# First two weight chunks computed together, bias rows and memory tokens handled earlier, two exponentials joined

## The chip, the cores and the metric

One core of a Trainium2 chip. The metric is the device time of one execution in microseconds; lower is better. A transformer trunk of four layers runs from HBM to HBM in one launch.

## What is computed

The reference is a trunk of four layers on 256 tokens of width 1024, all in float32. Cut to what the opening of the first layer does:

```python
p = x @ attn_w_in[j]                     # 1024 -> 3*768 + 256
q, k, v = jnp.split(p[..., :2304], 3, -1)
bias = table[_t5_bucket(k_pos[None, :] - q_pos[:, None])]
probs = jax.nn.softmax(q_h @ k_h.T + bias)      # 6 heads, 2 maps each
w = probs[:, 0] - lam * probs[:, 1]
km, vm = jnp.split(mem @ w_kv, 2, -1)           # 256 memory tokens
recalled = softmax(qx @ km.T) @ vm              # 4 memory heads
y = jnp.concatenate([mixed, recalled], -1) @ w_o[layer]
x = layer_norm(ALPHA * x + y)
f = conv_ffn(x); x = layer_norm(ALPHA * x + f)
```

Layers 1 and 2 replace the attention by a gated recurrence and by a short convolution; layer 3 is attention again.

## The kernel before

**Tiling.** Every projection is cut into chunks of 256 output columns (or, for `O` forms, 256 rows); one chunk is 1 MB of weights and two *units* of 128 x 1024 numbers. SP streams the units in order into a ring of five buffers, `raw` (line 341); `load_unit(u)` at 599 fills one. Each float32 operand is split in two: ACT rounds a unit to `w_hi` (`round_unit`, 1025 to 1030), DVE subtracts to get `w_lo` (`lo_unit`, 1261 to 1267). Each product is then three passes on TensorE: hi by hi, hi by lo, lo by hi. `x` and the memory tokens are split the same way, a quarter at a time ("cut", ACT 1141 to 1146, DVE 1425 to 1430), into `xT_hi`, `xT_lo`, `memT_hi`, `memT_lo`.

**Order.** `make_schedule` (64 to 230) writes one list of items by hand. Every engine walks the same list and does its own part of each item, in the order of the list, so an item that waits on an engine holds all later items of that engine. `chunk(...)` (83) puts in the rounding of a unit two chunks ahead, the first half of the products, what stands in `between`, the rounding of the next unit, the second half, what stands in `after`. The dictionary `at` says what goes where: `at[2n]` is between the halves of the n-th chunk after the first, `at[2n + 1]` behind its second half. In layer 0 the chunks are 0 `XQ` (memory queries), 1 and 2 `QK` (queries and keys of heads 0 and 1), 3 `KM` and 4 `VM` (keys and values of the memory), 5 and 6 `QK` of heads 2 and 3, and so on. Chunk c has units 2c and 2c + 1.

**The opening.** SP issues a quarter of x and a quarter of chunk 0 in turn, four times (603 to 607), then units 2 to 4, with two small tables (the one-hot matrix and the bias table) ahead of unit 4 (608 to 612). From unit 5 on (628 to 656) a load waits until the `w_lo` of the unit five before is done. Behind some of these loads stand others: the memory tokens `y_tok` (1 MB) behind unit 5, the small tables one by one behind units 8 to 14 (`load_small`), the last of them `lam_w`; a write of the bias rows to a scratch in HBM behind unit 11 and the spread load of `bias` behind unit 13, which waits for that write.

PE warms up with `WARM_UP` = 2 products of zeros (860 to 866). Chunk 0 is made quarter by quarter (758 to 772): each quarter needs its x and its weights ("begin", ACT 1147 to 1151, DVE 1431 to 1436). The first half of chunk 1 has its own form (773 to 781): all hi passes, then the lo pass. `bias_rows` (898 to 902 on PE, 1191 to 1194 on ACT) is one product of the bias table with the one-hot matrix, copied to SBUF by ACT; it uses a side bank of PSUM that chunk 2 uses next, so chunk 2 waits for ACT's copy (`side`, 667 to 672). Its place is between the halves of chunk 1, `at[0]`. The memory tokens are cut between the halves of chunk 2, `at[2]`; chunk 3 waits for all four quarters (line 695).

**Memory attention and first heads.** Both `xlog` items (memory logits, PE 903 to 913, maxima on DVE 1492 to 1509) stand between the halves of chunk 4, `at[6]`. `xexp` 0 (four exponentials on ACT, 1195 to 1208) stands behind chunk 4, `at[7]`; `xexp` 1 and then `xprob` 0 (DVE, 1510 to 1526) between the halves of chunk 5, `at[8]`. `log` 0 and `log` 1 (logits of two heads, PE 914 to 924, DVE with the bias 1499 to 1509) stand behind chunk 5, `at[9]`; they reuse the PSUM banks of the memory logits and so wait for `xexp` 0 and 1. `exp` 0, `xturn` 0 (memory probabilities turned on PE 925 to 937, copied by ACT 1209 to 1216) and `xprob` 1 are `at[10]`, between the halves of chunk 6; `exp` 1 and `xpv` 0 (memory values, PE 947 to 958, reads ACT's copies) are `at[11]`. The rounding of units 14 and 15 (chunk 7) stands around the first half of chunk 5. `prepare` (`at[5]`, DVE 1389 to 1418 with two exponentials on ACT) makes constants from all small tables and waits until the last has landed.

Of the kernel before, what the change touches and what calls it, by code (L numbers as in the profile page):

```python
# [25 lines left out]
P = 128  # L26
SEQ = 256
D = 1024
KT = D // P
# [34 lines left out]
def make_schedule():  # L64
# [40 lines left out]
    for q in range(4):  # L105
        items.extend([("cut", "x", q), ("begin", q)])
    for u in range(2, AHEAD):
        split_units(u)
    norms = 0
    for layer in range(DEPTH):  # L110
# [3 lines left out]
        if layer == 0:  # L114
            split_units(1 + AHEAD)
        if kind == "attn":
# [16 lines left out]
            if layer == 0:  # L133
# [5 lines left out]
                at[0], at[2] = [("bias_rows",)], [("cut", "mem", q) for q in range(4)]  # L139
                at[5] = [("prepare",)]  # L140
# [92 lines left out]
def trunk_kernel(nc, stream, x, x_t, mem_t, rel_bias, ln, lam, subln, lower, hnorm, cconv, fconv,  # L233
# [93 lines left out]
    with ExitStack() as ctx:  # L327
# [145 lines left out]
        first_landed = [sem("first_landed0"), sem("first_landed2")]  # L473
# [124 lines left out]
        def _(sp):  # L598
# [4 lines left out]
            for q in range(4):  # L603
                at = slice(q % 2 * 512, q % 2 * 512 + 512)
                sp.dma_start(x_tok[:, q // 2, at], xT_dram[:, q // 2, at]).then_inc(xT_landed[q], 16)
                sp.dma_start(raw[:, q // 2, at], stream[0, :, q * 512:(q + 1) * 512]).then_inc(
                    raw_landed[q // 2] if q % 2 else first_landed[q // 2], 16)
            for u in range(2, RAW):
                if u == RAW - 1:
                    for dst, src in small[:2]:  # L610
                        sp.dma_start(dst[:], src).then_inc(table_landed, 16)
                load_unit(u)
# [53 lines left out]
        def _(pe):  # L666
# [13 lines left out]

            def half(c, i, pos, begun=False):
# [6 lines left out]
                if (c, i) == (1, 0):  # L688
                    pe.wait_ge(hi_ready, 3)
                elif c:  # L690
# [67 lines left out]
                elif c == 0:  # L758

                    banks, every = [PROJ[0][:, j * SEQ:(j + 1) * SEQ] for j in range(2)], slice(0, SEQ)  # L760
                    for q in (2 * i, 2 * i + 1):
                        pe.wait_ge(*(hi_ready, i + 1) if q % 2 else (first_hi, i + 1))
                        for w, a, part in ((w_hi, a_hi, cut_hi), (w_hi, a_lo, cut_lo), (w_lo, a_hi, None)):
                            if part:
                                pe.wait_ge(part["x"], q + 1)
                            else:
                                pe.wait_ge(*(lo_ready, i + 1) if q % 2 else (first_lo, i + 1))
                            for k in (2 * q, 2 * q + 1):
                                for j in range(2):
                                    at = (k % 4 * 2 + j) * P  # L770
                                    last = pe.matmul(banks[j], w[:, slot, at:at + P], a(k, every), start=(part is cut_hi and k + j == 0),
                                                     stop=(w is w_lo and k == KT - 1), skip_group_check=True)
                elif (c, i) == (1, 0):

                    bank, every = PROJ[1][:, 0:SEQ], slice(0, SEQ)
                    for k in range(KT):
                        pe.matmul(bank, w_hi[:, slot, k * P:(k + 1) * P], a_hi(k, every), start=(k == 0), stop=False)
                        pe.matmul(bank, w_hi[:, slot, k * P:(k + 1) * P], a_lo(k, every), start=False, stop=False)
                    pe.wait_ge(lo_ready, 3)
                    for k in range(KT):  # L780
                        last = pe.matmul(bank, w_lo[:, slot, k * P:(k + 1) * P], a_hi(k, every), start=False, stop=(k == KT - 1))
# [927 lines left out]
```

## Time and profile before

| | |
|---|---|
| median of 3 runs | 1250.84 us (1249.69 to 1251.08) |
| the profiled execution | 1250.47 us, its span 1248.7 us |
| granted TensorE clock, mean | 0.998 of full speed |
| PE busy | 1235.7 us, 99% of the span |
| DVE busy | 1024.2 us, 82% |
| ACT busy | 729.7 us, 58% |
| DMA | 229 MB, mean 184 GB/s |

PE is TensorE's matmuls, PEld its weight loads, DVE VectorE, ACT ScalarE, SPq the queue of SyncE that issues the transfers. In a timeline row the columns are start and duration in us, engine, line, operation, output and inputs, shapes, count of merged instructions, and in brackets how long the engine stood idle before and what ended that. "issue" means that the profile shows nothing that the engine waited for. A matmul's end is modelled, so its duration includes the way through the array; the distance of starts is the pace.

### The profile page before, as it was taken

The numbers are of one execution on the slowest core, as the hardware profiler recorded it, in microseconds if no ns is written. First come the engines' busy times: TensorE is split into PE (matmuls) and PEld (weight loads), VectorE is DVE, ScalarE is ACT, GpSimd is POOL, SyncE is SP. The second block draws the span as 40 slices with busy tenths as digits, with TensorE's granted clock in tenths as the row PEclk, the third lists the DMA queues.
The fourth block names the chain that finished last, engine by engine and source line by source line (L and its number), as shares of the span: only waits on it lengthen the run. The fifth ranks groups of instructions, "written<-read, shape, count | busy, mean of one in ns | idle before, by whom it ended". The sixth has DMA issues, their size and how long they took to land.

```text
span 1248.7 us, 19664 instructions
## 1 busy us (share of the span) xinstructions
PE 1235.7 (99%) x7368; PEld 1082.9 (87%) x7368; DVE 1024.2 (82%) x1597; ACT 729.7 (58%) x1188; POOL 20.0 (2%) x29
## 2 busy tenths in 40 slices
PE   8999999999999999999999999999999999999997
PEld 6888888888999998888889888888888888888886
DVE  6776888888879888988888878988888776988887
ACT  6665755555776546655554545655554774755552
POOL 0000000000000000000000000000000000000000
PEclk9999999999999999999999999999999999999999
DMA  9744575556454345666555665665555533666651
GB/s 337 236 146 135 183 245 187 190 186 191 154 185 133 121 137 168 224 197 200 188 187 169 221 204 168 221 202 189 192 189 172 188 119 118 204 218 202 193 193 54
DMA packets 64106, 229.27 MB, mean 184 GB/s; under 512 B 7526, under 2 KB 9190, under 8 KB 62860
## 3 DMA queue, kind: packets, MB, share of 16 engines
q1 hardware_dynamic: 64012, 228.02, 55.6%
q8 instruction: 59, 0.97, 0.3%
q14 instruction: 35, 0.29, 0.1%
HBM read 226.93 MB, written 1.06 MB: 183 GB/s over the span
## 4 chain that ended last, share of the span: by engine, by line
PE 95%; DMA 2%; DVE 1%; ACT 1%; SPq 0%; issue 0%; DVEq 0%
PE pair L753 28%; PE acc L853 21%; PE pair L756 14%; PE pair L791 4%; PE pair L792 4%; PE pair L793 4%; PE acc L753 2%; PE acc L834 2%; PE acc L832 2%; PE acc L833 2%; PE pair L1012 2%; DMA raw<-in_stream 1%; PE pair L816 1%; PE pair L820 1%; PE pair L818 1%; PE acc L756 1%
## 5 line engine op out<-in xcount | busy, mean ns | idle before, releaser
L1266 DVE TENSOR_TENSOR w_lo<-raw,w_hi 128x1024 fp32r<-128x1024 f32 x402 | 485.3, 1222 | 108.7 <-ACT w_hi L1030 107.2
L1030 ACT ACTIVATE w_hi<-raw 128x1024 fp32r<-128x1024 f32 x402 | 422.7, 1058 | 216.5 <-PE pair L756 69.8
L753 PE MATMUL pair<-xT,w_hi 128*128 128x512 f32 x1520 | 478.3, 396 | 1.5 <-ACT bias_rows L1193 1.5
L756 PEld LDWEIGHTS pair<-xT,w_lo 128*128 128x128 f32 x1520 | 285.8, 188 | 66.8
L756 PE MATMUL pair<-xT,w_lo 128*128 128x256 f32 x1520 | 298.9, 278 | 0.0
L753 PEld LDWEIGHTS pair<-xT,w_hi 128*128 128x128 f32 x1520 | 233.9, 189 | 4.9 <-issue 2.0
L1077 ACT ACTIVATE hid<-pair 128x512 f32<-128x512 f32 x88 | 52.5, 596 | 125.0 <-PE pair L756 125.0
L791 PE MATMUL pair<-xT,w_hi 128*128 128x256 f32 x344 | 100.3, 292 | 0.0
L1307 DVE TENSOR_TENSOR hid<-pair,hid 128x512 f32<-128x512 f32 x88 | 60.7, 690 | 47.3 <-ACT hid L1077 47.2
L792 PE MATMUL pair<-xT,w_hi 128*128 128x256 f32 x344 | 97.4, 283 | 0.0
L793 PE MATMUL pair<-xT,w_lo 128*128 128x256 f32 x344 | 97.3, 283 | 0.0
L853 PE MATMUL acc<-w_hi,gT_hi 128*128 128x512 f32 x304 | 94.0, 391 | 0.0
L853 PE MATMUL acc<-w_hi,gT_lo 128*128 128x512 f32 x304 | 93.7, 389 | 0.0
L853 PE MATMUL acc<-w_lo,gT_hi 128*128 128x512 f32 x304 | 93.7, 389 | 0.0
L1130 ACT ACTIVATE cv<-hid,fconv_w 128x256 f32<-128x256 f32 x176 | 79.2, 499 | 16.3 <-DVE hid L1307 16.0
L1283 DVE SCALAR_TENSOR_TENSOR cv<-hid,fconv_w,cv 128x255 f32<-128x255 f32 x176 | 77.4, 481 | 3.1
L1279 DVE SCALAR_TENSOR_TENSOR cv<-hid,fconv_w,cv 128x255 f32<-128x255 f32 x176 | 77.0, 480 | 0.0
L791 PEld LDWEIGHTS pair<-xT,w_hi 128*128 128x128 f32 x344 | 65.8, 191 | 3.3 <-issue 3.0
L853 PEld LDWEIGHTS acc<-w_lo,gT_hi 128*128 128x128 f32 x304 | 57.1, 188 | 12.2
L853 PEld LDWEIGHTS acc<-w_hi,gT_lo 128*128 128x128 f32 x304 | 57.1, 188 | 11.8
L792 PEld LDWEIGHTS pair<-xT,w_hi 128*128 128x128 f32 x344 | 65.9, 192 | 0.0
L793 PEld LDWEIGHTS pair<-xT,w_lo 128*128 128x128 f32 x344 | 65.8, 191 | 0.0
(221 smaller groups left out, 1661.1 us busy)
## 6 DMA issues: line engine op xcount, KB each, us to landing
raw<-in_stream SPq DMA_DIRECT2D x402, 512.0 KB, 4.6
gains<-in_ln SPq DMA_DIRECT2D x8, 1024.0 KB, 8.3
bias<-bias_scratch SPq DMA_DIRECT2D x2, 1152.0 KB, 8.6
x_tok<-in_x_t SPq DMA_DIRECT2D x4, 256.0 KB, 5.2
raw<-in_stream SPq DMA_DIRECT2D x4, 256.0 KB, 5.4
y_tok<-in_mem_t SPq DMA_DIRECT2D x1, 1024.0 KB, 10.2
x_tok<-in_x SPq DMA_DIRECT2D x1, 1024.0 KB, 6.7
out<-x_tok SPq DMA_DIRECT2D x4, 256.0 KB, 2.0
```

What stands on the lines that cost most here:

```text
L753: pe.matmul(bank, w_hi[:, slot, kk * P:(kk + 1) * P], xT[:, kk].rearrange("p a s -> p (a s)"), start=(kk == 0), stop=(kk == KT - 1), skip_ ...
L756: last = pe.matmul(bank[:, 0:SEQ], w_lo[:, slot, kk * P:(kk + 1) * P], xT[:, kk, 0, :], start=False, stop=(kk == KT - 1), skip_group_check ...
L791: pe.matmul(bank, w_hi[:, slot, at], a_hi(k, every), start=(k == 0), stop=False)
L792: pe.matmul(bank, w_hi[:, slot, at], a_lo(k, every), start=False, stop=False)
L793: last = pe.matmul(bank, w_lo[:, slot, at], a_hi(k, every), start=False, stop=(k == KT - 1))
L853: last = pe.matmul(ACC[2 * t + h][:], b(i, tok), w[:, slot, h * 512:h * 512 + 512], start=False, stop=False, skip_group_check=True)
L1030: nc.scalar.activation(w_hi[:, u % SPLIT, :], raw[:, u % RAW, :], ACT.Copy).then_inc(hi_ready, 1)
L1130: last = nc.scalar.activation(cv[:, w, i, :], hid[:, w, i, :], ACT.Copy, scale=fconv_w[:, layer, 1, first + i:first + i + 1])
L1266: v.tensor_tensor(w_lo[:, u % SPLIT, :], raw[:, u % RAW, :], w_hi[:, u % SPLIT, :].bitcast(F32), ALU.subtract).then_inc(lo_ready, 1)
L1279: last = v.scalar_tensor_tensor(dst[i][:, 1:SEQ], src[i][:, 0:SEQ - 1], weights(0, i), dst[i][:, 1:SEQ], ALU.mult, ALU.add)
L1283: last = v.scalar_tensor_tensor(dst[i][:, 0:SEQ - 1], src[i][:, 1:SEQ], weights(2, i), dst[i][:, 0:SEQ - 1], ALU.mult, ALU.add)
L1307: v.tensor_tensor(hid[:, w], PAIR[proj_ord[c] % 2][:, :, 0:SEQ], hid[:, w], ALU.add).then_inc(hid_ready, 1)
```

## The change

The units of chunks 0 and 1 are laid out anew: unit 0 holds the first half of the inner dimension of chunk 0, unit 1 that of chunk 1, units 2 and 3 the second halves. SP issues, for each quarter of x, that quarter and two quarter loads (256 KB each), one of each chunk; the two small tables follow all twelve, then unit 4. ACT and DVE cut x and round both quarters as they come. PE makes the products of a quarter for chunk 0 and chunk 1 in turn; the last quarter of chunk 1 falls in chunk 1's own halves. One warm-up product of half width is added. `bias_rows` stands ahead of chunk 1's first half, behind the rounding of unit 5. The memory tokens are cut behind chunk 1, ahead of the rounding of unit 8. `xexp` 1 stands directly behind `xexp` 0, ahead of the rounding of unit 14.

```diff
     for q in range(4):
-        items.extend([("cut", "x", q), ("begin", q)])
-    for u in range(2, AHEAD):
-        split_units(u)
+        items.extend([("cut", "x", q), ("begin", q, 0), ("begin", q, 1)])
...
             split_units(1 + AHEAD)
+            items.append(("bias_rows",))
...
-                at[0], at[2] = [("bias_rows",)], [("cut", "mem", q) for q in range(4)]
-                at[5] = [("prepare",)]
+                at[1], at[5] = [("cut", "mem", q) for q in range(4)], [("prepare",)]
+                at[8].remove(it("xexp", 1))
+                at[7].append(it("xexp", 1))
...
                 sp.dma_start(x_tok[:, q // 2, at], xT_dram[:, q // 2, at]).then_inc(xT_landed[q], 16)
-                sp.dma_start(raw[:, q // 2, at], stream[0, :, q * 512:(q + 1) * 512]).then_inc(
-                    raw_landed[q // 2] if q % 2 else first_landed[q // 2], 16)
-            for u in range(2, RAW):
-                if u == RAW - 1:
-                    for dst, src in small[:2]:
-                        sp.dma_start(dst[:], src).then_inc(table_landed, 16)
+                for u in (q // 2 * 2, q // 2 * 2 + 1):
+                    sp.dma_start(raw[:, u, at], stream[u // 2, :, u % 2 * UNIT + at.start:u % 2 * UNIT + at.stop]).then_inc(
+                        raw_landed[u] if q % 2 else first_landed[u], 16)
+            for dst, src in small[:2]:
+                sp.dma_start(dst[:], src).then_inc(table_landed, 16)
+            for u in range(4, RAW):
                 load_unit(u)
...
+            HI, LO = [(w_hi, xT_hi), (w_hi, xT_lo)], [(w_lo, xT_hi)]
+
+            def first_products(q, b, w, a):
+
+                slot, n = 2 * (q // 2) + b, 2 * (q // 2) + b + 1
+                if w is w_lo:
+                    pe.wait_ge(*(lo_ready, n) if q % 2 else (first_lo, n))
+                else:
+                    pe.wait_ge(*(hi_ready, n) if q % 2 else (first_hi, n))
+                    pe.wait_ge((cut_hi if a is xT_hi else cut_lo)["x"], q + 1)
+                for k in (2 * q, 2 * q + 1):
+                    for j in range(2):
+                        at = (k % 4 * 2 + j) * P
+                        last = pe.matmul(PROJ[b][:, j * SEQ:(j + 1) * SEQ], w[:, slot, at:at + P], a[:, k, :],
+                                         start=(w is w_hi and a is xT_hi and k + j == 0),
+                                         stop=(w is w_lo and k == KT - 1), skip_group_check=True)
+                return last
...
+                elif c < 2:
+
+                    for q, b in {(0, 0): [(0, 0), (0, 1), (1, 0), (1, 1)], (0, 1): [(2, 0), (2, 1), (3, 0)], (1, 0): [(3, 1)],
+                                 (1, 1): [(3, 1)]}[c, i]:
+                        for w, a in {(1, 0): HI, (1, 1): LO}.get((c, i), HI + LO):
+                            last = first_products(q, b, w, a)
...
             idle_work(WARM_UP)
+            pe.matmul(ACC[0][:, 0:SEQ], zeros[:, 0:P], zeros[:, 0:SEQ], start=True, stop=True)
...
-                    u, h = item[1] // 2, item[1] % 2
+                    u, h = item[1] // 2 * 2 + item[2], item[1] % 2
```

The last edit stands on ACT and on DVE; the two old forms of the first chunks' products (lines 758 to 781) go, and the layout of the stream on the host follows.

## Rows read from the trace of the kernel before

**Rows 1.** The page, part 4: the chain of work that ended last, by engine

```profile
PE 95%; DMA 2%; DVE 1%; ACT 1%; SPq 0%; issue 0%; DVEq 0%
```

**Rows 2.** All waits of PE over the span: total us, times, longest

```profile
PE pair L771 <- ACT w_hi L1151: 1.8, 3, 0.9
PE pair L753 <- ACT bias_rows L1193: 1.5, 1, 1.5
...
PE pair L791 <- issue: 1.0, 1, 1.0
PE acc L921 <- ACT ex L1205: 0.5, 1, 0.5
```

**Rows 3.** Timeline of PE, 0 to 60 us

```profile
1.51 3.78 PE L863 MATMUL acc<-zeros 128*128 128x512 f32 x4 [1.51 <-DVE zeros L1422]
...
22.32 0.70 PE L753 MATMUL pair<-xT,w_hi 128*128 128x512 f32 x2 [1.53 <-ACT bias_rows L1193]
...
29.17 0.36 PE L791 MATMUL pair<-memT_hi,w_hi 128*128 128x256 f32 x1 [1.04 <-issue]
...
50.20 1.13 PE L921 MATMUL acc<-qk 64*128 64x256 f32 x8 [0.53 <-ACT ex L1205]
...
58.07 1.08 PE L955 MATMUL pair<-xprobT,vm 128*64 128x256 f32 x8
```

**Rows 4.** Timeline of ACT, 12 to 60 us

```profile
14.11 1.06 ACT L1030 ACTIVATE w_hi<-raw 128x1024 fp32r<-128x1024 f32 x1 [0.51 <-DMA raw<-in_stream]
...
20.65 1.06 ACT L1030 ACTIVATE w_hi<-raw 128x1024 fp32r<-128x1024 f32 x1 [2.56 <-DMA raw<-in_stream]
...
22.85 1.06 ACT L1030 ACTIVATE w_hi<-raw 128x1024 fp32r<-128x1024 f32 x1 [0.67 <-DMA raw<-in_stream]
...
47.16 1.07 ACT L1030 ACTIVATE w_hi<-raw 128x1024 fp32r<-128x1024 f32 x1
48.11 0.48 ACT L1205 ACTIVATE ex<-acc,neg_max 128x256 f32<-128x256 f32 x1
...
49.91 1.09 ACT L1030 ACTIVATE w_hi<-raw 128x1024 fp32r<-128x1024 f32 x1
...
54.59 0.51 ACT L1205 ACTIVATE ex<-lg,neg_max 128x256 f32<-128x256 f32 x1 [2.10 <-DVE neg_max L1509]
...
56.58 1.06 ACT L1215 ACTIVATE xprobT<-pair 128x512 f32<-128x512 f32 x2
```

**Rows 5.** Windows: us, busy of PE, PEld, DVE, ACT, POOL, PEclk, DMA share, GB/s

```profile
4.00:6.00 2.00, 1.29 (x2) 0.00 (x0) 0.69 (x1) 1.11 (x2) 0.00 (x0) 1.00 0.86 192
6.00:8.00 2.00, 1.70 (x12) 1.50 (x12) 1.30 (x2) 1.36 (x3) 0.00 (x0) 1.00 1.01 371
14.00:16.00 2.00, 2.00 (x19) 2.00 (x18) 1.65 (x2) 1.46 (x2) 0.00 (x0) 1.00 1.05 418
18.00:36.00 18.00, 15.43 (x113) 14.37 (x112) 11.47 (x13) 10.34 (x17) 0.00 (x0) 1.00 1.03 369
```

**Rows 6.** Timeline of SP's queue, 20 to 45 us

```profile
26.69 0.33 SPq L600 DMA_DIRECT2D raw<-in_stream  x1
...
30.61 0.71 SPq L619 DMA_DIRECT2D lam_w<-in_lam  x1
```

**Rows 7.** Timeline of DVE, 20 to 54 us

```profile
23.94 1.23 DVE L1266 TENSOR_TENSOR w_lo<-raw,w_hi 128x1024 fp32r<-128x1024 f32 x1 [0.98 <-ACT w_hi L1030]
...
26.58 2.49 DVE L1430 TENSOR_TENSOR memT_lo<-y_tok,memT_hi 128x512 fp32r<-128x512 f32 x4
...
38.87 0.69 DVE L1392 CAST masks<-masks_in 128x1024 uint8<-128x1024 f32 x1 [4.18 <-DMA lam_w<-in_lam]
...
48.27 1.23 DVE L1266 TENSOR_TENSOR w_lo<-raw,w_hi 128x1024 fp32r<-128x1024 f32 x1 [0.42 <-ACT w_hi L1030]
...
51.03 1.23 DVE L1266 TENSOR_TENSOR w_lo<-raw,w_hi 128x1024 fp32r<-128x1024 f32 x1 [0.19 <-ACT w_hi L1030]
```

**Rows 8.** The chain of work in order of time: start us, us, what

```profile
51.65 0.12 PE pair L792
```

More of the change, by code:

```diff
@@ L472, in trunk_kernel @@
         xT_landed = [sem(f"xT_landed{q}") for q in range(4)]
-        first_landed = [sem("first_landed0"), sem("first_landed2")]
+        first_landed = [sem(f"first_landed{u}") for u in range(4)]
         cut_hi, cut_lo = [{"x": sem(f"x_{name}"), "mem": sem(f"mem_{name}")} for name in ("hi", "lo")]
@@ L686, in half @@
                 held = form == "O" and index[0] == chunks_of_sum - 2
-                if (c, i) == (1, 0):
-                    pe.wait_ge(hi_ready, 3)
-                elif c:
+                if c > 1:
                     pe.wait_ge(lo_ready, 2 * c + (2 if final or c in early else i + 1))
@@ L757, in half @@
                                              start=False, stop=(kk == KT - 1), skip_group_check=True)
[L758 to L781, printed above, removed]
+                elif c < 2:
[3 more added lines that the diff above has]
+                            last = first_products(q, b, w, a)
                 elif form == "F":
@@ L1431, in _ @@
                 elif name == "begin":
-                    u, h = item[1] // 2, item[1] % 2
+                    u, h = item[1] // 2 * 2 + item[2], item[1] % 2
                     at = slice(h * 512, h * 512 + 512)
@@ L1647, in stream_layout @@
         cols = {"QK": (P * index, MIX + P * index), "CG": (MIX + P * index, 2 * MIX + P * index)}.get(role)
-        if c == 0:
-            stream[c] = w[:, col:col + 256].reshape(KT, P, 256).transpose(1, 0, 2).reshape(P, 2 * UNIT)
+        if c < 2:
+            for i, first in enumerate(cols or (col, col + P)):
+                block = w[:, first:first + P].reshape(2, KT // 2, P, P).transpose(2, 0, 1, 3)
+                for h in range(2):
+                    stream[h].reshape(P, 2, KT // 2, 2, P)[:, c, :, i] = block[:, h]
             continue
```

## The prediction

> **What bounds the kernel now.** The page comes first. Its chain of the work that ended last is 95% TensorE (PE) [rows 1], so what a change is worth is how much PE idle time it takes out or puts in. The list of what PE waited for, over the whole span, names few places [rows 2]: the first products wait for rounded weights (1.8 us in three waits), chunk 2 for the copy of the bias rows (1.5), chunk 3 for "issue" (1.0), and the second set of head logits for an exponential (0.5). The last of these places is at 50.20, so PE runs without a wait from there to the end, and a microsecond won or lost ahead of it arrives whole. The edits touch only this opening, and the four lines hold 4.8 us, so about 5 us (0.4%) is all there is to win.
>
> PE's own timeline gives their places: 1.53 us before 22.32, 1.04 before 29.17, 0.53 before 50.20 [rows 3]. Then the other engines are read over the same stretch, and they decide. ACT rounds unit 6 at 20.65 and unit 7 at 22.85, both the moment their transfers land [rows 4]; the DMA engines are full from 18 to 36 us (share 1.03) [rows 5]. SP issues lam_w, the last small table, at 30.61 [rows 6], and DVE, which needs all small tables for "prepare", stands 4.18 us until it lands at 38.87 [rows 7]. Unit 12's low part and the memory logits' maxima stand behind "prepare" in DVE's order, the exponentials on ACT behind the maxima, the probabilities on DVE behind those. **From 38.87 to about 58 us a DVE-and-ACT chain that starts with a DMA landing runs close under PE.** It touches PE at 50.20 and stays just hidden at 58.07 (no wait is shown there).
>
> **The change, part by part.**
>
> *First two chunks together.* No product is added or removed; 96 of 0.12 us each [rows 8] are reordered so that each quarter of x feeds 24 instead of 12. ACT and DVE trade two whole-unit roundings for four half-unit ones each. SP issues four 256 KB transfers in place of two of 512 KB. All transfers keep their place by bytes in the one queue, so the last quarter lands about where unit 3 landed, 14.11 [rows 4]. From there 24 products (2.9 us) and the bias product put the start of chunk 2 at about 18.5 to 19, against 22.32: some 3.5 us earlier.
>
> The unshown price is that of one megabyte fetched in 2 KB pieces. Upper bound: the rate at which the first quarters crawled, 192 GB/s from 4 to 6 us, against 418 later with larger pieces: 5.5 minus 2.5 us, 3.0 later. Lower bound: a gain of 0.3, as I see no row that excludes finer pieces getting through sooner. The nearest row is 6 to 8 us, where quarters alone moved at 371: 2.8 minus 2.5, **0.3 us later** [rows 5]. I take that, since the four pieces come after this stretch; everything behind them in the queue shifts with them, lam_w too.
>
> *One more warm-up product*, half as wide: a quarter of the 3.78 us that the two present ones take, 0.95 [rows 3]. It lies in the idle time of 0.9 before the first product [rows 2]; without that cover it would cost 0.95.
>
> *Bias rows right behind.* ACT's copy no longer stands behind unit 6's landing (20.65). It comes after unit 5's rounding, so the 1.53 us of PE go. What is late next is chunk 3.
>
> *Memory tokens half a chunk sooner.* ACT's four roundings move ahead of unit 8's, to right behind unit 7's and one copy; they cannot pass unit 7, which lands at 22.85 [rows 4]. DVE takes unit 7's low part at 23.94 as now and follows at once with the four memory parts (2.49 us) instead of starting them at 26.58 [rows 7]: ready at 23.94 + 1.23 + 2.49 = 27.66 against 29.07 now. Chunk 3 starts at about 27.8 instead of 29.17: **1.41 us** is left of the 3.5. The move is paid by unit 8: its low part, now done when the memory parts start, is done at 28.9, and SP's next load goes from 26.69 to about 28.9 [rows 6]. I cost that at nothing because transfers queued ahead of it keep the engines busy (share 1.03 from 18 to 36) [rows 5]; without that backlog it would delay lam_w by up to 2.2. SP's scratch write and bias load stay behind the same unit loads.
>
> So PE comes to the head logits 1.41 us early. But lam_w's landing is set by bytes, not by PE. Without the last part PE would wait for the second memory exponential until 50.20 as now, and the gain would be zero.
>
> *Two exponentials joined.* ACT now does exp 0, unit 14's rounding (47.16), exp 1 (48.11), unit 15 (49.91) [rows 4]. Swapped, exp 1 starts at 47.16 and the second logits are released 0.95 sooner, at about 49.25. But unit 14's rounding falls behind the four exponentials, from 47.16 to 48.96 (the four take 49.91 minus 48.11, 1.80). DVE's next instruction in order is unit 14's low part, and it already waits 0.42 for ACT there [rows 7]. Its start goes from 48.27 to 50.07. Behind it in DVE's order stand the first probabilities, unit 15's low part (51.03, which gives 0.19 of its own wait back, and 0.08 more goes in the spacing), the QK sums and the head logits' maxima; they come 1.53 later. ACT's next exponential waits for those maxima (2.10 idle before 54.59) and so goes to 56.12; the copy of the turned probabilities behind it, 56.58 with 1.06 us, ends at 57.64 + 1.53 = 59.17 [rows 4]. PE needs it for the first memory values, at 58.07 now [rows 3], and would be there at 57.1 with the 0.95 won. The hand-over from ACT to PE lies between 0 and 0.29 (ACT's next start after exp 1, 49.91, to PE's 50.20); with 0.14 PE starts at 59.31, **1.24 us later than now**, after 2.2 us of idle. Behind that I see no further wait: from there ACT and DVE are late by 1.53 and PE by 1.24, so what lies under PE now by more than 0.3 us still does, and the list has no wait there [rows 2].
>
> **Sum.** Early gain 3.5, cut to 1.41 at chunk 3, to 0.95 at the second logits, and to minus 1.24 at the memory values; plus 0.3 of DMA: 1.54 us later. The profiled execution took 1250.47 (span 1248.7): 1252.0. The runs' median, 1250.84, stands 0.37 above it, so I forecast **1252.3**. That is 0.12% slower, within the 0.2% (2.5 us) that a measurement of this kernel can tell from no change.
>
> **Rivals.**
>
> *The opening's gain stays (faster).* If the chain behind 38.87 moves forward, because lam_w lands earlier, the end follows it down to PE's own pace: 1.41 gives 1249.4, and if the memory rounding does not bind chunk 3 either, 3.5 gives 1247.3. It decides once lam_w lands 2.7 us sooner (1.24 plus 1.41), by 36.2. For it: SP's waits before that issue hang on DVE. Against: the queue is full, and the order of the bytes does not change [rows 5]. Chance 0.12 for the first, 0.10 for the second.
>
> *The opening's transfers come later (slower).* Place: the twelve quarters. Price: up to 3.0 us, as above, passed whole to lam_w and so to the memory values: 1250.84 + 1.24 + 3.0 = 1255.1; from 1.3 us of delay on, the change is slower by over 0.2%. For it: 192 GB/s at 4 to 6 us. Against: 371 right after [rows 5]. Chance 0.10. The Trainium skill, "DMA: Bandwidth & Descriptors", section "Rules for kernel authors", asks for a megabyte or more per transfer; by it the halved transfers speak against this part.
>
> *The clock falls at a wait.* The new waits (about 3 us before chunk 3, 2.2 at the memory values) are longer than any in the list, and the granted clock stood at 1.00 through the 1.53 and 1.04 [rows 5]. If it fell to the lower of its two levels, 1.2 GHz, at the second, 24 products of the next unit would take twice their 0.12: 2.9 more, 1255.2. Chance 0.06. The Trainium skill, "TensorE: Matmul & The Clock Gate", section "Why this matters for your kernels", warns of such a drop after idle time between bursts; no row here shows one ahead of the tail.
>
> *It does not bind.* If unit 14's delay is absorbed (probabilities earlier than I think), the 0.95 stands: 1249.9. Chance 0.10.
>
> **How the numbers follow.** My chain has 0.52: 1251.6 to 1253.2, DMA from minus 0.4 to plus 1.1. With the rivals: faster by over 0.2% is 0.10 (the 3.5 case), slower by over 0.2% 0.16 (the two slow cases), same 0.74. The range 1248.9 to 1254.0 leaves out the 3.5 case and the upper parts of the two slow ones, below 0.2.
>
> **What would show it.** In the profile after: PE's idle time before chunk 2 gone; chunk 3 released by the last memory low part at 27.7, after about 3 us of idle; lam_w landing at 38.9 to 39.2; exp 1 directly behind exp 0; DVE idle 2.2 us before unit 14's low part; a new PE wait of about 2.2 us at L955 for ACT's copy L1215 near 59. If L955 shows no wait, the last step is wrong; if lam_w lands more than 2 us off, the DMA step is; if PE idles elsewhere after 60 us, I have missed a consumer.

## The result, and the profile after

The changed kernel takes 1254.55 us (median of 9 runs, 1253.3 to 1255.85) against 1250.84 for the kernel before: a ratio of 1.003 [1.0022, 1.0038], slower by 0.3%. The forecast was 1252.3 with a range up to 1254.0: the direction was right, the size was not. The forecast was 1.5 us slower than before; the change is 3.7 slower and lies above the range. The profiled execution took 1254.9 (span 1253.1, against 1248.7 before).

All waits of PE in the changed kernel (total us, times, longest):

```profile
PE acc L920 <- ACT ex L1204: 2.4, 2, 1.7
PE pair L789 <- issue: 2.3, 1, 2.3
PE acc L861 <- DVE zeros L1421: 1.5, 1, 1.5
```

The three waits for the first weights and the wait for the bias rows [rows 2] are gone, as intended. What is left are 2.3 us ahead of chunk 3 and 2.4 at the two head logits, the one place where the list of before had only 0.5. No wait is listed for the memory values, where I had put the loss. PE's timeline gives the places (start, us, engine, line, [idle before, releaser]):

```profile
18.86 0.66 PE L769 MATMUL pair<-xT,w_hi 128*128 128x512 f32 x2
...
26.93 0.46 PE L789 MATMUL pair<-memT_hi,w_hi 128*128 128x256 f32 x1 [2.31 <-issue]
...
34.25 0.28 PE L814 MATMUL pair<-w_hi,memT_hi 128*128 128x256 f32 x1
...
49.54 1.14 PE L920 MATMUL acc<-qk 64*128 64x256 f32 x8 [1.69 <-ACT ex L1204]
51.37 2.08 PE L920 MATMUL acc<-qk 64*128 64x256 f32 x8 [0.69 <-ACT ex L1204]
53.37 0.58 PE L789 MATMUL pair<-xT,w_hi 128*128 128x256 f32 x1
...
58.26 1.04 PE L934 MATMUL pair<-ident,prob 128*128 128x128 f32 x8
...
62.10 1.08 PE L954 MATMUL pair<-xprobT,vm 128*64 128x256 f32 x8
```

The start of chunk 4, and the start and end of the first half of chunk 6, in the kernel before:

```profile
35.00 0.28 PE L816 MATMUL pair<-w_hi,memT_hi 128*128 128x256 f32 x1
...
51.26 0.39 PE L791 MATMUL pair<-xT,w_hi 128*128 128x256 f32 x1
...
54.24 1.03 PE L935 MATMUL pair<-ident,prob 128*128 128x128 f32 x8
```

Against [rows 3], chunk 2 starts 3.46 earlier (18.86, was 22.32), chunk 3 2.24 earlier (26.93, was 29.17), and the memory values come 4.03 later (62.10, was 58.07). The last of these is nearly the whole 4.4 by which the spans differ. So the stretch from 27 to 62 us lost 6.3. The products show that not all of it is waiting: chunk 3 takes 7.32 from its start to that of chunk 4 (34.25), and took 5.83 before (29.17 to 35.00); the second set of logits takes 2.08 where the first takes 1.14; the first half of chunk 6 takes 4.89 (53.37 to 58.26), and took 2.98. The windows of the same trace show why (stretch, its length, busy time of PE, PEld, DVE, ACT and POOL, granted clock, DMA share, GB/s):

```profile
24.00:27.00 3.00, 0.69 (x5) 0.47 (x3) 3.00 (x6) 3.00 (x6) 0.00 (x0) 1.00 1.04 399
27.00:30.00 3.00, 3.00 (x15) 3.00 (x16) 3.00 (x5) 2.29 (x4) 0.00 (x0) 0.50 0.94 336
30.00:32.00 2.00, 2.00 (x17) 2.00 (x17) 0.92 (x1) 0.37 (x1) 0.00 (x0) 0.89 0.91 265
32.00:34.00 2.00, 2.00 (x19) 2.00 (x18) 1.23 (x1) 0.69 (x1) 0.00 (x0) 1.00 0.92 253
...
50.00:52.00 2.00, 1.31 (x11) 0.88 (x10) 0.00 (x0) 2.00 (x7) 0.00 (x0) 0.73 0.43 139
52.00:54.00 2.00, 2.00 (x11) 1.29 (x8) 1.77 (x3) 2.00 (x5) 0.00 (x0) 0.50 0.34 123
54.00:56.00 2.00, 2.00 (x11) 2.00 (x11) 2.00 (x3) 0.60 (x1) 0.00 (x0) 0.50 0.68 215
```

Two things are to be seen. The granted clock is at 0.50, the lower of its two levels (1.2 instead of 2.4 GHz), right behind each of the two places where PE stood; in the kernel before it was 1.00 in both stretches (for the first, [rows 5]). And the DMA engines, which I had taken to be full until 36 us (1.03) [rows 5], work at 0.91 to 0.94 of their time from 27 to 34. SP's, DVE's and ACT's timelines give the rest of the picture (the first line is of the kernel before, the others of the changed one):

```profile
29.19 0.38 SPq L625 DMA_DIRECT2D bias<-bias_scratch  x1
```

```profile
28.02 0.33 SPq L600 DMA_DIRECT2D raw<-in_stream  x1
...
29.87 0.38 SPq L625 DMA_DIRECT2D bias<-bias_scratch  x1
...
30.88 0.43 SPq L619 DMA_DIRECT2D lam_w<-in_lam  x1
```

```profile
40.99 0.70 DVE L1391 CAST masks<-masks_in 128x1024 uint8<-128x1024 f32 x1 [7.03 <-DMA lam_w<-in_lam]
...
52.20 1.23 DVE L1265 TENSOR_TENSOR w_lo<-raw,w_hi 128x1024 fp32r<-128x1024 f32 x1 [2.24 <-ACT w_hi L1029]
```

```profile
58.24 0.51 ACT L1204 ACTIVATE ex<-lg,neg_max 128x256 f32<-128x256 f32 x1 [3.64 <-DVE neg_max L1508]
```

Unit 13 is issued 1.33 later than in [rows 6]; lam_w is issued only 0.27 later but lands 2.1 later: DVE's "prepare" begins at 40.99 instead of 38.87 [rows 7]. The 2.24 before unit 14's low part is the wait the forecast gave to the join (2.2). The first head exponential starts at 58.24. That is 54.59 [rows 4], plus the 1.53 of the join, plus the 2.12 of lam_w. So the chain is the one forecast, moved by lam_w's landing. It holds in all other profiles with the loads in their old order, except prepare_late, which moves "prepare" itself: 54.59, plus 1.53 where the exponentials are joined, plus the lateness of "prepare", gives the first head exponential to within 0.01.

### The profile page after: what moved, and what is told of

Same layout as the page of the kernel before. It is cut to its first block, busy times and chain, and to the rows that moved or that the text cites. A ratio compares the mean times of both kernels' runs of the same rounds, so it can differ in the third digit from the quotient of the medians.

```text
span 1253.1 us, 19685 instructions
## 1 busy us (share of the span) xinstructions
PE 1240.3 (99%) x7370; PEld 1087.2 (87%) x7370; DVE 1024.3 (82%) x1599; ACT 730.3 (58%) x1190; POOL 20.1 (2%) x29
## 3 DMA queue, kind: packets, MB, share of 16 engines
HBM read 226.93 MB, written 1.06 MB: 182 GB/s over the span
## 4 chain that ended last, share of the span: by engine, by line
PE 95%; DMA 2%; DVE 1%; ACT 0%; SPq 0%; issue 0%; DVEq 0%; ACTq 0%
PE pair L769 28%; PE acc L851 21%; PE pair L772 14%; PE pair L789 4%; PE pair L790 4%; PE pair L791 4%; PE acc L769 2%; PE acc L830 2%; PE acc L832 2%; PE acc L831 2%; PE pair L1011 2%; PE acc L920 1%; PE pair L814 1%; PE pair L816 1%; PE pair L818 1%; PE acc L772 1%
## 5 line engine op out<-in xcount | busy, mean ns | idle before, releaser
L789 PE MATMUL pair<-xT,w_hi 128*128 128x256 f32 x336 | 98.8, 294 | 0.0
L790 PE MATMUL pair<-xT,w_hi 128*128 128x256 f32 x336 | 95.8, 285 | 0.0
```

Source lines behind the costliest of these rows:

```text
L789: pe.matmul(bank, w_hi[:, slot, at], a_hi(k, every), start=(k == 0), stop=False)
L790: pe.matmul(bank, w_hi[:, slot, at], a_lo(k, every), start=False, stop=False)
```

## The experiments

The open points were: does lam_w's landing cause the second loss; what moved lam_w; what does the clock cost; and is the join's own price right. Each kernel was timed beside runs of the kernel before on the same chip (medians 1250.52, 1250.28 and 1250.27 in the three timed groups; one run of 1251.51 beside most of the kernels that ran once). Between kernels of different groups the difference of medians is given, and where it matters that of the ratios.

**Is it lam_w?** The changed kernel with lam_w moved up in SP's order:

```diff
-                    load_small(2 + u - RAW - 3)
+                    if 2 + u - RAW - 3 < len(small):
+                        load_small(2 + u - RAW - 3)
...
                 if u == RAW + 8:
+                    load_small(len(small))
                     sp.wait_ge(rows_out, 16)
```

> The changed kernel with one load moved in SP's order: lam_w is issued behind unit 13 and ahead of the wait for rows_out and the bias load, instead of behind unit 14. My theory: the second loss of the changed kernel (PE's 2.4 us before the two head logits, and the half clock from 50.9 to 57.7 behind it) comes from the DVE, which stands 7.0 us at the preparation of the small tables until lam_w lands at 40.96. Then lam_w lands by about 34, the DVE's wait is under 1 us, the memory exponentials begin near 43.3 behind the eviction of chunk 4 (47.5 in the changed kernel), the first head logits near 48.2 without a wait, and the clock stays at 1.0 there: 2.4 of waiting and about 2.9 of half clock go, 1249 to 1250. The wait ahead of chunk 3 and the half clock from 27.0 to 30.4 stay. Rival: the order on ACT sets the exponentials, lam_w is only the last of several: they begin at 45 or later and the time stays above 1252. Second rival: the bias, 0.9 later, holds the head maxima: a new DVE wait on the bias near 50, 1252.

1248.48 us (10 runs), ratio to the kernel before 0.9985 [0.9976, 0.9994], 6.1 below the changed kernel (5.6 by the two ratios) and a little better than expected. From its trace, the wait of DVE, the head logits and all waits of PE:

```profile
34.49 0.69 DVE L1393 CAST masks<-masks_in 128x1024 uint8<-128x1024 f32 x1 [0.35 <-DMA lam_w<-in_lam]
```

```profile
47.96 2.00 PE L922 MATMUL acc<-qk 64*128 64x256 f32 x16
```

```profile
PE pair L791 <- issue: 2.1, 1, 2.1
PE acc L863 <- DVE zeros L1423: 1.5, 1, 1.5
PE pair L956 <- ACT xprobT L1216: 0.2, 1, 0.2
```

One load of 256 KB, issued ahead of the bias and unit 14 instead of behind them, takes the DVE's wait from 7.03 to 0.35, both sets of logits run without a wait, and the clock stays at 1.00 there. The wait and the half clock ahead of chunk 3 are still in this kernel. That lam_w causes the second loss, the wait at the logits and the half clock behind it, is shown. The 6.1 is more than the price of its being 2.1 late, as lam_w lands 4.4 earlier here than in the kernel before; there the same move gains 0.8 (last experiment). The Trainium skill, "DMA: Bandwidth & Descriptors", section "Queues, rings and completion order", says that the DMA engines take each ring's work in order. These two traces agree: issued behind the bias lam_w lands at 40.96, issued ahead of it at 34.47.

Another way round the same wait is to move "prepare" in place of lam_w:

```diff
-                at[1], at[5] = [("cut", "mem", q) for q in range(4)], [("prepare",)]
+                at[1] = [("cut", "mem", q) for q in range(4)]
...
                 at[7].append(it("xexp", 1))
+                at[8].append(("prepare",))
```

> The changed kernel with the item that waits for lam_w (prepare) behind the first probabilities, between the halves of chunk 5, instead of behind chunk 3. Theory A (DVE's wait for lam_w is what holds the opening's gain): PE has no wait at the logits, chunk 6 starts at about 49.9 instead of 53.4 (and 51.26 before), lam_w still lands near 41, and the time is about 1249.4. If the chain behind prepare is not what binds: no change, 1254 to 1255.

1253.39, ratio 1.0022 [1.0013, 1.0031], and not the 1249.4 expected: the logits' wait is gone (chunk 6 at 50.18), but two new ones stand behind it.

```profile
56.25 0.66 PE L935 MATMUL pair<-ident,prob 128*128 128x128 f32 x4 [2.49 <-DVE qk L1299]
...
61.05 1.08 PE L955 MATMUL pair<-xprobT,vm 128*64 128x256 f32 x8 [1.28 <-ACT xprobT L1215]
```

"prepare" keeps DVE for 3.8 us (50.50 to 54.31 here; 40.99 to 44.80 in the changed kernel), and behind its new place stood the sums of chunk 5 that free the bank for the turned probabilities. The wait at the head of DVE's order could be moved behind other work, but not for nothing.

**What moved lam_w?** First the memory cut: put back in its old place in the changed kernel (mem_back), and moved ahead alone in the kernel before (mem_alone). lam_w came late in both, which no single cause explains; so both ran once more, as did the changed kernel and the kernel before (the names with _again are a second profile of the same kernel), and the opening ran without cut and join (quarters_bias).

mem_back, from the changed kernel:

```diff
-                at[1], at[5] = [("cut", "mem", q) for q in range(4)], [("prepare",)]
+                at[2], at[5] = [("cut", "mem", q) for q in range(4)], [("prepare",)]
```

mem_alone, from the kernel before:

```diff
-                at[0], at[2] = [("bias_rows",)], [("cut", "mem", q) for q in range(4)]
+                at[0], at[1] = [("bias_rows",)], [("cut", "mem", q) for q in range(4)]
```

quarters_bias, from mem_back:

```diff
-                at[8].remove(it("xexp", 1))
-                at[7].append(it("xexp", 1))
```

> The changed kernel with the memory tokens cut between the halves of chunk 2 again. Theory A (the memory move pushes unit 8's low part and with it SP's load of unit 13 back, the transfer engines run dry, lam_w lands 2.1 us later): lam_w is back at 38.9 us, SP's load of unit 13 back at 26.7; the joined exponentials still cost 1.2, so about 1252.1 in all, although chunk 3 starts no earlier than before (29.2). Rival B (the twelve quarter loads of the opening, or chance, delay lam_w): lam_w stays near 41 and the time near 1254.5.

> The kernel before with the memory move alone (behind chunk 1). Theory A: SP's load of unit 13 goes from 26.7 to 28 or later, lam_w lands at 40 to 41 instead of 38.9, the second logits are released 1 to 2 us later than 50.20, and the kernel is slower, 1252 to 1253. Rival B: lam_w at 38.9, second logits at 50.2, 1250.8.

> The changed kernel with the memory cut back in its old place, a second look. If the quarters of the opening hold the later transfers up, lam_w lands at 40 or later again although unit 13 is issued near 26; if the 40.6 of the first look was chance, it lands at 39 to 39.5 (the bias 0.3 later than in the kernel before), and the time of such a run is near 1251.

> The opening by quarters and the bias rows behind the first chunk alone, without the cut and without the join. lam_w as in mem_back_again: 39 to 39.5 if the opening moves it by no more than its own 0.3, 40 or later if it is the opening. Chunk 3 waits about 3.8, as the cut stands in its old place.

> The kernel before with the memory cut moved ahead alone, a second look. If the move makes unit 13 wait for the low part of unit 8 and leaves the transfers idle from 29 to 30, lam_w lands at 40.3 to 41 again; if that was chance, near 38.9.

> The changed kernel, unchanged, a second look. lam_w at 40 to 41, PE waiting about 2.3 before chunk 3 and 1.5 to 2.5 before the head logits, and the clock at half for one stretch behind each of the two waits: the first as long as in the first profile (3.4), the second 3.4 or 6.8.

> The kernel before, unchanged, for a second look at where lam_w lands. If the place of the loads in the queue sets it, it lands within 0.4 of 38.9 again and the bias is issued near 29.2. If its landing scatters from run to run by a microsecond or two, it may be anywhere from 38.5 to 41, and a part of the 2.1 us between the two kernels' profiles is chance.

Start of "prepare" on DVE, which is lam_w's landing to within 0.1 us, in the profiles with the loads in their old order (join_alone, exps_apart and filled are described further below; prepare_late is left out, where lam_w landed at 40.98, and mem_at_bias, where the cut stands still further ahead, with 39.82):

| | memory cut in its old place | memory cut ahead |
|---|---|---|
| opening as before | 38.87 (before), 38.79 (before_again), 38.34 (join_alone) | 40.80 (mem_alone), 40.30 (mem_alone_again) |
| opening by quarters | 40.60 (mem_back), 39.20 (mem_back_again), 39.41 (quarters_bias) | 40.99 (the change), 39.54 (after_again), 39.89 (exps_apart), 40.52 (filled) |

The cut moved ahead is enough by itself: both profiles of mem_alone are 1.4 to 2.5 later than all three of its row without it. The windows of mem_alone show the DMA engines partly idle:

```profile
28.00:30.00 2.00, 2.00 (x17) 1.86 (x16) 2.00 (x2) 1.47 (x4) 0.00 (x0) 1.00 0.59 217
30.00:32.00 2.00, 2.00 (x19) 2.00 (x18) 1.93 (x4) 0.83 (x1) 0.00 (x0) 1.00 0.82 251
32.00:34.00 2.00, 2.00 (x19) 2.00 (x18) 0.83 (x2) 1.06 (x1) 0.00 (x0) 1.00 0.78 230
```

Unit 13 is issued at 29.02 (was 26.69 [rows 6]), since it waits for the low part of unit 8, which now stands behind the four memory parts on DVE. The engines are busy for 0.59 of the two microseconds ahead of 30, where they had 1.03 in the kernel before, and what follows comes later. Time: mem_alone 1252.62, ratio 1.0021 [1.0011, 1.0031], as expected of the cut as cause.

In the changed kernel putting the cut back did not bring lam_w back to 38.9, against the expectation: the opening by quarters moves it too, by 0.3 to 0.5 in two of three profiles and by 1.7 in the third, with unit 13 issued early (25.70 to 27.43). The DMA engines are full from 28 to 32 in the two later profiles (1.04 and more in mem_back_again, 1.00 and more in quarters_bias) and at 0.88 from 30 to 32 in mem_back. What makes these three late was not settled: the bias is issued 0.3 to 0.6 later (29.52 to 29.83, was 29.19), since it waits for its rows to come back from HBM, and in mem_back lam_w itself took 3.95 us from the start of its first packet to the end of its last (before: 2.86). mem_back took 1253.09, ratio 1.0015 [1.0005, 1.0025]: it loses more at chunk 3, for which PE waits 3.8 and 4.7 (quarters_bias 4.8). The kernels that ran once took 1252.40 (mem_back_again), 1252.23 (quarters_bias), 1254.64 (mem_alone_again) and 1250.30 (before_again).

The landing is the end of the last of 128 packets of 2 KB, and the traces hold every packet. The median packet scatters less: it starts at 36.64, 36.55 and 36.20 in the upper left of the table, at 38.47 and 37.86 in the upper right, at 37.43, 37.11 and 37.34 in the lower left, and at 38.06, 38.09, 37.45 and 37.93 in the lower right. By this measure each of the two edits delays lam_w in every profile, the cut alone by 1.2 to 2.3 and the quarters alone by 0.5 to 1.2; with both it is 0.8 to 1.9, so the two do not add up.

The second profile of the changed kernel is the most telling of the single ones. lam_w was expected at 40 to 41; it landed at 39.5, only 0.7 late, though its median packet came as late as in the first profile (38.09 and 38.06), and the run took 1252.72:

```profile
39.54 0.69 DVE L1391 CAST masks<-masks_in 128x1024 uint8<-128x1024 f32 x1 [4.82 <-DMA lam_w<-in_lam]
```

```profile
56.79 0.51 ACT L1204 ACTIVATE ex<-lg,neg_max 128x256 f32<-128x256 f32 x1 [3.64 <-DVE neg_max L1508]
```

```profile
PE pair L954 <- ACT xprobT L1214: 1.3, 1, 1.3
PE pair L934 <- DVE qk L1298: 0.6, 1, 0.6
PE acc L920 <- ACT ex L1204: 0.2, 1, 0.2
```

This is the forecast's chain: 54.59 + 1.53 + 0.67 is 56.79, and PE waits at the memory values for ACT's copy of the turned probabilities, as written. What changes between the two executions of one kernel is when lam_w lands, and with it how long PE stands at the logits; PE also comes 0.8 later to chunk 3 (27.69), which leaves it less to wait for.

**What does the clock cost?** Four more products of zeros between chunk 2 and chunk 3:

```diff
+                if (c, i) == (3, 0):
+                    idle_work(4)
                 if c > 1:
```

> The changed kernel with four more products of zeros (128x512, into a bank that nothing reads) between chunk 2 and chunk 3, inside the 2.3 us in which PE waits for the memory tokens: nothing else moves. Theory: the granted clock fell to half at 27.0 because PE stood still before it; with the fillers it stays at 1.0 there, chunk 3 starts at 26.9 as before and ends 1.7 us sooner. If lam_w at 40.96 decides the second stretch alone, these 1.7 are waited away before the head logits and the time stays at 1254 to 1255; if the clock's cost adds up with the rest, the time is 1252.5 to 1253.2. Rival: the clock falls all the same (it is not the idle stretch), nothing changes.

1253.53, ratio 1.0027 [1.0017, 1.0036], 1.0 below the changed kernel by the medians and 0.4 by the ratios, whose intervals overlap: a gain in time is not shown. What the clock did is. The fillers' group and two windows of this trace:

```profile
24.79 3.60 PE L863 MATMUL acc<-zeros 128*128 128x512 f32 x8
```

```profile
26.00:28.00 2.00, 2.00 (x7) 0.95 (x5) 2.00 (x3) 1.51 (x2) 0.00 (x0) 1.00 1.05 387
28.00:30.00 2.00, 2.00 (x16) 1.77 (x15) 1.68 (x4) 1.61 (x4) 0.00 (x0) 1.00 1.01 362
```

With PE kept at work the clock stays at 1.00 where it had been 0.50, so the fall belongs to the idle stretch. The fillers were too long (chunk 3 starts at 27.83, 0.9 later than in the changed kernel), so what the fall costs chunk 3 is better read from its length: 7.32 against 5.83, 1.5 us. The second fall, behind the logits, stays in this kernel, shorter: from 50.96 to 54.37. The Trainium skill, "TensorE: Matmul & The Clock Gate", section "Why this matters for your kernels", warns of throughput lost after idle gaps between bursts of products; these traces agree that a gap can do it. It need not: in prepare_late the 2.49 us before 56.25 were followed by a clock of 1.00:

```profile
54.00:56.00 2.00, 0.00 (x0) 0.00 (x0) 1.95 (x5) 1.43 (x3) 0.00 (x0) 1.00 0.00 0
56.00:58.00 2.00, 1.75 (x15) 1.75 (x16) 1.97 (x11) 0.13 (x1) 0.00 (x0) 1.00 0.64 152
```

**Where should the memory cut stand?** ACT stands idle from 18.7 to 20.8 in the changed kernel, and the memory has landed at 19.5:

```diff
             items.append(("bias_rows",))
+            items.extend([("cut", "mem", q) for q in range(4)])
...
-                at[1], at[5] = [("cut", "mem", q) for q in range(4)], [("prepare",)]
+                at[5] = [("prepare",)]
```

> The changed kernel with the cut of the memory tokens one place further ahead: directly behind the bias rows, before unit 6 is rounded, where ACT stands idle from 18.7 to 20.8 and the memory has landed (19.5). Theory on the first loss: chunk 3 then starts at about 24.6, straight behind chunk 2, without the 2.3 us of waiting and without the half clock from 27.0 to 30.4 (3.4 us at half clock, 1.7 given back), 4.0 in all by the start of chunk 5; unit 13 is loaded at about 26.5 instead of 28.0. What comes of it at the end depends on lam_w. If lam_w lands late only because unit 13 and what stands behind it were issued late, it lands near 39 as in the kernel before, and the time is 1249.5 to 1251. If it still lands at 40.5 to 41, the memory exponentials don't move, the 4.0 are waited away before the head logits (6 us there instead of 2.4), and the time is 1252.5 to 1254.5.

> Both edits together: the memory tokens cut directly behind the bias rows, and lam_w loaded ahead of the bias. If the two losses are what I think and nothing else stands behind them, neither the 2.3 us ahead of chunk 3 nor the 2.4 us before the head logits is left, the clock stays at 1.0 from 6.5 on, and against the changed kernel 2.3 + 1.7 + 2.4 + 2.9 = 9.3 go at most; what the next late thing takes back (the DVE's sums behind the preparation, the turned probabilities for the memory values) I put at 1 to 2: 1245.5 to 1247.5, faster than both kernels. Rival: the transfers set the pace of the first 60 us, then the 4 us won at chunk 3 come back as waits for units 11 to 15 and the time is 1249 to 1251.

Alone it gives 1253.64, ratio 1.0025 [1.0015, 1.0034], which was expected only for a landing at 40.5 to 41: chunk 3 starts at 25.60 without a wait and at full clock, "prepare" at 39.82, and PE waits the gain away:

```profile
48.37 3.90 PE L921 MATMUL acc<-qk 64*128 64x256 f32 x16 [3.40 <-ACT ex L1205]
```

lam_w is still 0.95 late here, although unit 13 is issued at 27.46 (28.02 in the changed kernel), and the DMA engines are full from 26 to 36 (1.02 and more in every window of 2 us), so idle DMA engines are not its only cause.

Together with the early lam_w it is 1247.11 (8 runs), ratio 0.9973 [0.9962, 0.9984]. The waits of PE that are left:

```profile
PE acc L864 <- DVE zeros L1424: 1.5, 1, 1.5
PE pair L957 <- ACT xprobT L1217: 1.1, 1, 1.1
```

**The join.** Taken back in the changed kernel, made alone in the kernel before, and taken back where nothing else holds the chain. The diff is in each case these two lines (added instead of taken out in join_alone):

```diff
-                at[8].remove(it("xexp", 1))
-                at[7].append(it("xexp", 1))
```

> The changed kernel with the two exponentials apart as before. Theory A with my chain: lam_w stays at 41, the second logits wait until about 52.3 (50.20 plus 2.1), unit 14's low part is no longer held, the head's exponential starts at about 56.7 instead of 58.24, and the memory values at about 60.2 plus what the clock takes: 1253 to 1254. If joining costs nothing (rival C): no difference from 1254.55 beyond the second logits coming 0.95 later, about 1255.5.

> The kernel before with the join alone (the second memory exponential moved one step ahead, so that unit 14 is rounded behind both). By my prediction's step: unit 14's low part 1.8 later, the head exponentials 1.53 later (56.1), the second logits no later than before, the memory values up to 1.2 later: 1251 to 1252. Rival: lam_w decides (the join moves nothing ahead of its landing), within 0.5 of the kernel before.

> The kernel with both early edits (memory tokens cut behind the bias rows, lam_w ahead of the bias) with the two memory exponentials apart again, as in the kernel before: unit 14 is rounded between them. It tests the join's own term by my prediction (the head exponentials 1.53 later) where lam_w is out of the way. From the joined twin's trace: first exponential 40.0 to 41.9, unit 14 rounded to 42.9, second exponential to 44.7, which is before the second head logits need their banks (45.2), so no wait there; the low part of unit 14 at about 42.9 instead of 44.8, the head maxima and the first head exponentials about 1.5 earlier (49.3 instead of 50.8), and the 1.1 us that PE waits for the turned probabilities goes: 1245.7 to 1246.4 against 1247.1. Rival: the join costs nothing, the time stays at 1247.1; or the second logits wait about 1.4 and it is 1247.4 to 1248.

exps_apart took 1255.12 (1251.91 to 1257.65, 7 runs), which against 1254.55 tells nothing. Its profile is of the fastest of these runs. There lam_w is earlier (39.89), and PE waits 0.39 and 1.64 at the logits and not at the memory values (59.07). join_alone took 1251.23, ratio 1.0008 [0.9999, 1.0017], 0.96 above its runs of the kernel before; the interval just includes no change. Its first head exponential and PE's new wait:

```profile
55.58 0.51 ACT L1207 ACTIVATE ex<-lg,neg_max 128x256 f32<-128x256 f32 x1 [3.64 <-DVE neg_max L1511]
```

```profile
PE pair L957 <- ACT xprobT L1217: 1.3, 1, 1.3
```

The copy of the turned probabilities is late by what the forecast gave it, and the wait at the logits [rows 2] is gone. both_apart took 1246.05 (1245.29 to 1246.21, 4 runs), ratio 0.9963 [0.9948, 0.9978], 1.06 below its joined twin (the runs of the two do not meet: 1246.21 at most here, 1246.82 at least there; the intervals of the ratios do). PE waits nowhere behind the opening:

```profile
PE acc L862 <- DVE zeros L1422: 1.5, 1, 1.5
PE pair L695 <- ACT w_hi L1151: 0.5, 1, 0.5
```

This version, the new opening with lam_w and the memory cut earlier and without the join, is the fastest of all, 0.37% below the kernel before.

**Was lam_w binding before as well?** The same move of the load in the kernel before:

> The kernel before with lam_w issued behind unit 13 and ahead of the bias. Its wait before the head logits was only 0.5. If lam_w at 38.9 was what held it there too, the preparation begins near 34, the memory exponentials near 44 instead of 45.4, the 0.5 goes and no more: 1249.8 to 1250.4; and where runs of the kernel before take 1252 to 1253 because lam_w came later by chance, those are gone. Rival: nothing moves, as the order on ACT sets the exponentials.

1249.47, ratio 0.9993 [0.9983, 1.0003]; "prepare" starts at 35.31, the wait of 0.5 at the logits is gone, and the runs lie between 1248.9 and 1250.42, where those of the kernel before reach 1252.25. The median is 0.8 lower, but the interval includes no change: at most a little was to be won, and most of lam_w's lateness was hidden, as the forecast said.

## Why the prediction was wrong, point by point

- *Start of chunk 2*: forecast 18.5 to 19, 3.5 earlier; measured 18.86, 3.46 earlier. Right here; the profile is on the early side, as ten others with this opening lie between 18.60 and 19.58, most of them at 19.2 to 19.3 (mem_at_bias, where PE waits for the bias rows again, has 19.95).
- *Quarters*: forecast 0.3 later for all transfers behind them. In the first profile units 10 to 13 landed 0.5 to 0.6 earlier than before (unit 13 at 32.23, was 32.87), but that profile is the odd one: unit 11 landed at 29.63 there and at 30.08 to 31.02 in the eleven others with this opening, against 29.76 to 30.80 in the six with the old one. The medians, 30.70 and 30.26, are 0.4 apart: about the forecast's term. For lam_w the quarters cost 0.3 to 0.5 in two of three profiles and 1.7 in the third.
- *Bias rows*: the wait is gone. Right.
- *Chunk 3*: forecast 27.8, a gain of 1.41; measured 26.93, a gain of 2.24, because unit 7 is rounded at 22.11 instead of 22.85 [rows 4]. The second profile, with unit 7 rounded at 22.86, has 27.69: the step was right.
- **The step that failed**: "I cost that at nothing because transfers queued ahead of it keep the engines busy". The later load of unit 13 was found and sized (up to 2.2 on lam_w), and then covered by a backlog that was read off one share (1.03 from 18 to 36) in the kernel before. The sum had lam_w 0.3 late; in the profile it is 2.12 late. mem_alone shows that the step fails without any other edit: with the cut alone unit 13 is issued 2.33 later, the DMA engines drop to 0.59, and lam_w lands 1.4 to 2.5 later. In the changed kernel the cut is not the only cause: the opening by quarters has a share, and mem_at_bias has lam_w 0.95 late with full engines. How the 2.12 divides is open. By the windows, idle time of the DMA engines from 27 to 34 is only about 0.5 us (an estimate from the shares 0.94, 0.91 and 0.92). Unit 13 itself lands earlier than before, and the lateness shows behind it, at the bias (37.73, was 36.20) and unit 14 (40.00, was 37.45).
- *Join*: forecast 1.24 later at the memory values, for 1.53 later at the head exponentials. Measured 0.96 (join_alone, not quite clear of noise) and 1.06 (both_apart against both_early) in time, and the 1.53 to within 0.01 in the chain. The mechanism was right and the term about right.
- *Where the loss shows*: forecast a wait of 2.2 at L955. Measured 1.3 there where lam_w is 0.7 late (after_again), and none where it is 2.1 late: PE stands at the logits instead and comes late to L954 by itself.
- *Clock*: the rival with 0.06 came true twice, but not at the memory values, where it was priced: behind chunk 3's wait, which I had named and not priced, and behind the logits, where I expected no wait. It costs chunk 3 1.5 (7.32 against 5.83) and the first half of chunk 6 1.9 (53.37 to 58.26, 4.89; before, 2.98 from 51.26). How much of the first is left at the end is not shown (filled), as PE waits at the logits behind it.
- *Rival "the opening's gain stays"*: it said that lam_w decides, and gave 1249.4 and 1247.3. With lam_w early the kernel takes 1248.48, and with the memory cut out of the way too, 1247.11. As a mechanism it was right, and it needed one more edit.
- *Rival "the opening's transfers come later"*: in part. lam_w came later by 1.7 in one of three profiles with the cut in its old place, beyond the 1.3 it named, and by 0.3 to 0.5 in the other two.
- *Rival "it does not bind"*: no; the 1.53 is in every profile with the join and the old order of the loads.

The sum, redone with measured terms: 1.24 for the join, 2.12 for lam_w, and 0.7 for PE's own lateness (the copy ends at 60.23 + 1.06 = 61.29, 61.4 with the hand-over; PE, slowed by the wait and the half clock, starts at 62.10) make 4.06; measured 4.03 at the memory values and 4.4 in the spans. The 0.7 is what is left over, not a term measured by itself. The forecast's own sum comes to 1252.4; it was written as 1252.3.

## What to carry to other kernels

When an edit delays an issue and you cover it with "the queue is full", ask how long the queue would last without that issue: a full share does not tell. Here an issue 2.3 us later was enough to leave the engines partly idle (mem_alone). A small load that one engine waits for at the head of its order belongs ahead of the large ones in the queue; this was worth 6.1 us in the changed kernel. And ask of every new idle stretch of PE what the clock behind it will be; a wait of 2.3 us cost 1.5 more here.

## What the runs showed of the hardware that was not expected

- The granted clock fell to half at each of eight waits of 2.1 to 4.8 us ahead of chunk 3, and at the logits with waits of 1.69 and 0.69 us close together. It stayed at 1.00 behind the 2.49 us of prepare_late, and behind 0.96 and 1.64 in mem_alone, whose second profile, with 1.40 and 1.64, shows it at half from 50.8 to 57.7. Which idle stretch is followed by half clock could not be told from its length alone.
- The landing of the same load in the same kernel, by the start of "prepare", differs by 1.45 us between two executions (40.99 and 39.54) and by 1.4 in mem_back (40.60, 39.20), while the kernel before repeats within 0.1 (38.87, 38.79). In the changed kernel the 1.45 lies in the load's last packets: the median packet starts at 38.06 and 38.09. A single profile of such a kernel can put that much on the wrong account.
